# Convolution's layer norm: channel sums by a matrix of ones, and other banks for the memory's first values

## The chip, the cores and the metric

The kernel runs on one core of a Trainium2 chip. The metric is the device time of one execution in microseconds (us), the median over several runs.

## What is computed

Three blocks are applied to an activation of 512 tokens by 1024 channels, held transposed (channels on partitions, eight tiles of 128 by 512). The first block has a mixer, an attention over 256 memory rows, and a gated feed-forward net; the second has four feed-forward nets, a pooling mixer and a latent attention. The change lies in the mixer of the first block. The part that matters, cut:

```python
def parallel_mixer(h, w_in, conv_dw, conv_dw_b, conv_ln_g, conv_ln_b, q_norm_g, k_norm_g, w_out, tabs):
    z = jnp.einsum("bsd,dc->bsc", h, w_in)
    ...
    a = a_val * jax.nn.sigmoid(a_gate)
    a = dwconv_centred(a, conv_dw, conv_dw_b)     # 512 channels, 31 taps
    a = layernorm(a, conv_ln_g, conv_ln_b)        # over the 512 channels of a token
    a = jax.nn.silu(a)
    ...
    att = gqa_blocked(q, k, v)
    mixed = jnp.concatenate([a, att], axis=-1)
    return jnp.einsum("bsc,cd->bsd", mixed, w_out)

def layernorm(x, g, b):
    mu = jnp.mean(xf, axis=-1, keepdims=True)
    var = jnp.mean(jnp.square(xf - mu), axis=-1, keepdims=True)
    y = (xf - mu) * lax.rsqrt(var + EPS)
    return (y * g + b)
```

The memory attention that follows needs `kv = mem_n @ w_mem_kv`; its second half, the values, is made in two halves of 512 columns, the first of them inside the stretch that the change touches.

## The kernel before

**Arithmetic.** Each product with weights is made in three passes, high by high, high by low and low by high (`mm3`, L380 to L382), on fp32r tiles. Weights come as units of at most 128 by 1024. SyncE fetches a unit (`raw`), ScalarE makes its high part (`wh`, `high`, L364), VectorE its low part (`wl`, `low`, L372), and TensorE uses it. There are three buffers for each of `raw`, `wh` and `wl`: the high part of unit i waits until unit i-3 has been used, the fetch of unit i until the low part of unit i-3 is made. Units of w_mem_kv's value half 0 are v0 to v3 here; w_out's first units follow them, and are called w_out0 and w_out1 here.

**Order.** Nothing is scheduled dynamically. Each engine runs one list, in the order in which the functions `..._tensor`, `..._scalar`, `..._vector` and `..._gpsimd` are called in `program`, with semaphore waits between engines (`sig.at`, `sig.up`). A `Ring` hands out buffers or PSUM banks in turn, and a `take` names what must have freed the slot. The eight banks are main (0 to 2), score (3, 4), turn (5, 6) and out (7).

**Stages around the change.** `attend_*` runs the mixer's attention. Its last steps (t = 33 to 37) transpose the exponents of the last head (`value_turn_tensor`, L992), split them on ScalarE (L1001) and VectorE (L1006), and multiply them by the values (`value_tensor`). Beside that VectorE makes one tap of the convolution in each step (`tap_vector`, L626, the sums in bank 7), the last one being the last tap of channel tile 1; channel tiles 2 and 3 get their last taps on ScalarE and GpSimd (L638, L645). `value_vector` (L1057) divides the last output tile and so frees its main bank.

Then comes `layernorm_*`. `cv` holds the convolution's output, four tiles of 128 channels by 512 tokens. TensorE works on `mem_value_tensor(0, kk)`, one unit of the memory's values at a time, and between them on the layer norm: sums of `cv` with the data as the stationary operand and one column of ones moving (L1177), which gives token sums on partitions; VectorE adds and scales them (L1209, L1212); `spread_rows` (L474) transposes them back to a row for all partitions; VectorE subtracts (L1217, "centred"); ScalarE squares (L433); GpSimd adds two of the squares to the first (`add_square`, L438); `square_sums` (L449, L450) sums over channels; `mean_square` (L457) and `inverse_root` (L464, `ALU.pow` with exponent -0.5) work on 128 by 4 numbers; `spread_rows` again; VectorE multiplies (L1227), ScalarE does the Silu and the high part (L1200, L1202), VectorE the low part (L1231).

`post_product_tensor` then multiplies the eight mixed tiles by w_out. Its first step, `linear_pair`, goes over the eight tiles with w_out0 and w_out1 side by side, so from its first tile on it needs the low parts of both units; tiles 0 to 3 are the attention's, tiles 4 to 7 the convolution's.

Of the kernel before, what the change touches and what calls it, by code (L numbers as in the profile page):

```python
# [9 lines left out]
ALU = mybir.AluOpType  # L10
# [195 lines left out]
def f(ap):  # L206
    return ap.bitcast(F32)


def build(nc, wts, xT, memT, pos, cols, ident_d, perm_d, rope_d, pool_d, mask_d, out):  # L210
    with ExitStack() as ctx:
# [853 lines left out]
        def value_gpsimd(e, j):  # L1065
            e.wait_ge(*sig.at(("atth", j)))
            e.tensor_tensor(hxl[:, j, :], att_turn.of(("att", j))[:, :], f(hxh[:, j, :]), ALU.subtract) \
                .then_inc(*sig.up("att_low", ("mixed", j), ("free", ("att", j))))

        def attend_tensor(e):  # L1070
            for t in range(TURNS + 6):
                now, before = value_turn(t), value_turn(t - 1)
                if now:
                    value_turn_tensor(e, *now)
                if t < TURNS:
                    mix_score_tensor(e, t)
                if now and now[1] == 3 and now[0] % 2 == 1:
                    divisor_rows_tensor(e, now[0] // 2)
                if before:
                    value_tensor(e, *before)  # L1080
                if t < 5:
                    mem_key_tensor(e, 3 + t)

        def attend_scalar(e):
            k = 9
# [51 lines left out]
        def mem_value_tensor(e, half, kk):  # L1137
            i = U_VAL[half][kk]
            h, lo = weights_of(i)
            if kk == 0:  # L1140
                for tt in range(2):
                    _, old = mainb.take(("mv", half, tt))
                    e.wait_ge(*sig.at(old))
            e.wait_ge(*sig.at(("low", i)))
            for tt in range(2):
                b = mainb.of(("mv", half, tt))
                for k in range(2):
                    sh, sl, ready = mem_src(2 * kk + k)
                    e.wait_ge(*sig.at(ready))
                    made = mm3(e, b[:, :], (sh[:, tt * P:(tt + 1) * P], sl[:, tt * P:(tt + 1) * P]), (h[:, k, :], lo[:, k, :]),  # L1150
                               kk == 0 and k == 0, kk == 3 and k == 1)
            made.then_inc(*sig.up("unit_done", ("unit", i)))

        def mem_value_scalar(e, half):
            r = slice(half * 512, half * 512 + 512)
            e.wait_ge(*sig.at(("unit", U_VAL[half][3])))
            e.wait_ge(*sig.at(("score", TURNS - 1)))
            for tt in range(2):
                e.activation(mv_h[:, tt, r], mainb.of(("mv", half, tt))[:, :], ACT.Copy).then_inc(*sig.up("mem_value_high", ("mvh", half, tt)))

        def mem_value_vector(e, half):
            r = slice(half * 512, half * 512 + 512)
            for tt in range(2):
                e.wait_ge(*sig.at(("mvh", half, tt)))
                e.tensor_tensor(mv_l[:, tt, r], mainb.of(("mv", half, tt))[:, :], f(mv_h[:, tt, r]), ALU.subtract) \
                    .then_inc(*sig.up("mem_value_low", ("mv", half, tt), ("free", ("mv", half, tt))))

        CONV_LAST = [("tap", c, CONV_K - 1) for c in range(4)]

        def layernorm_tensor(e):  # L1170
            mem_value_tensor(e, 0, 0)
            o, old = turnb.take("conv mean")
            e.wait_ge(*sig.at(old))
            for c in range(4):
                e.wait_ge(*sig.at(CONV_LAST[c]))
                for i in range(4):
                    made = e.matmul(o[:, 4 * i + c:4 * i + c + 1], cv[:, c, i * P:(i + 1) * P], ones[:, 0:1], start=True, stop=True)  # L1177
            made.then_inc(*sig.up("conv_sums", "conv sums"))
            mem_value_tensor(e, 0, 1)
            spread_rows(e, "conv mean", "conv mean")  # L1180
            mem_value_tensor(e, 0, 2)
            square_sums(e, "conv", 3)
            spread_rows(e, "conv", ("root", "conv"))
            mem_value_tensor(e, 0, 3)

        def layernorm_scalar(e):
            for kk in range(2):
                high(e, U_VAL[0][kk] + 2)
            for c in range(4):
                square(e, "conv", c, cv[:, c, :], ("centred", c))  # L1190
            high(e, U_VAL[0][2] + 2)
            high(e, U_VAL[0][3] + 2)
            mem_value_scalar(e, 0)
            e.wait_ge(*sig.at(("free", ("pm", 6))))
            e.wait_ge(*sig.at(("free", ("pm", 7))))
            for c in range(4):
                s, old = silu_turn.take(("silu", c))
                e.wait_ge(*sig.at(old))
                e.wait_ge(*sig.at(("lnorm", c)))
                e.activation(s[:, :], cv[:, c, :], ACT.Silu, scale=col("conv_ln_g", c), bias=col("conv_ln_b", c)).then_inc(*sig.up("conv_silu", ("silu", c)))  # L1200
                e.wait_ge(*sig.at(("silu", c)))
                e.activation(hxh[:, 4 + c, :], s[:, :], ACT.Copy).then_inc(*sig.up("conv_high", ("convh", c)))  # L1202

        def layernorm_vector(e):
            low(e, U_VAL[0][0] + 2)
            st, old = stats.take(("st", "conv mean"))
            e.wait_ge(*sig.at(old))
            e.wait_ge(*sig.at("conv sums"))
            e.tensor_reduce(st[:, 0:4], turnb.of("conv mean")[:, 0:16].rearrange("p (i c) -> p i c", i=4), AX.X, ALU.add) \  # L1209
                .then_inc(*sig.up("conv_mean", "conv summed", ("free", "conv mean")))  # L1210
            e.wait_ge(*sig.at("conv summed"))
            e.tensor_scalar(st[:, 48:52], st[:, 0:4], 1.0 / S, None, ALU.mult).then_inc(*sig.up("conv_mean", "conv mean"))  # L1212
            low(e, U_VAL[0][1] + 2)
            for c in range(4):
                e.wait_ge(*sig.at(("rows", "conv mean")))
                e.wait_ge(*sig.at(CONV_LAST[c]))
                e.tensor_tensor(cv[:, c, :], cv[:, c, :], turnb.of(("rows", "conv mean"))[:, :], ALU.subtract) \  # L1217
                    .then_inc(*sig.up("centred", ("centred", c), *([("free", ("rows", "conv mean"))] if c == 3 else [])))
            low(e, U_VAL[0][2] + 2)
            mean_square(e, "conv", 1.0 / S)  # L1220
            low(e, U_VAL[0][3] + 2)
            mem_value_vector(e, 0)
            for c in range(4):
                e.wait_ge(*sig.at(("rows", "conv")))
                e.wait_ge(*sig.at(("sq", "conv", 3)))
                e.wait_ge(*sig.at(("centred", c)))
                e.tensor_tensor(cv[:, c, :], cv[:, c, :], turnb.of(("rows", "conv"))[:, :], ALU.mult) \  # L1227
                    .then_inc(*sig.up("conv_normed", ("lnorm", c), *([("free", ("rows", "conv"))] if c == 3 else [])))
            for c in range(4):
                e.wait_ge(*sig.at(("convh", c)))  # L1230
                e.tensor_tensor(hxl[:, 4 + c, :], silu_turn.of(("silu", c))[:, :], f(hxh[:, 4 + c, :]), ALU.subtract) \  # L1231
                    .then_inc(*sig.up("conv_low", ("mixed", 4 + c), ("free", ("silu", c))))

        def layernorm_gpsimd(e):
            for k in (1, 2):
                add_square(e, "conv", k)
            inverse_root(e, "conv")

# [1515 lines left out]
```

## Time and profile before

| | us |
|---|---|
| median of 3 runs (lowest, highest) | 2621.32 (2616.62, 2622.31) |
| profiled execution, whole time | 2623.71 |
| profiled execution, span from the first to the last instruction | 2622.4 |
| TensorE busy | 2566.9 |
| VectorE busy | 1225.3 |
| ScalarE busy | 934.4 |
| GpSimd busy | 620.9 |

Times in the profile are from the start of the span. Ends of matmuls are modelled and overlap the next matmul's start, so the distance between two starts is the better measure of what a matmul costs in a row of them. The stretch of the change goes from about 212 us to 262 us. In the profile PE is TensorE, DVE VectorE, ACT ScalarE, POOL GpSimd, PEclk the granted TensorE clock as a share of full speed.

### The profile page before, as it was taken

Reading aid. Unit: us, or ns where it says so; the run is one execution under the profiler, and the core shown is the slowest. Engines: PE = TensorE matmul, PEld = TensorE weight load, DVE = VectorE, ACT = ScalarE, POOL = GpSimd, SP = SyncE. Lnnn points to the kernel's source line nnn. Section 1 sums busy time; section 2 is a strip of 40 time slices with the busy share of each in tenths; the row PEclk is TensorE's granted clock in tenths of the full one; section 3 lists DMA queues with packets and bytes.
Section 4 is the critical chain, followed back from the end, with each engine's and each line's share of the span. In section 5 each row is a group of like instructions: output and inputs, shape, how many; then the busy total and the mean of one; then the engine's idle time right before and its main releaser. Section 6 shows DMA issues by size and latency. Waiting matters only on the chain.

```text
span 2622.4 us, 28823 instructions
## 1 busy us (share of the span) xinstructions
PE 2566.9 (98%) x11706; PEld 2097.2 (80%) x11706; DVE 1225.3 (47%) x1613; ACT 934.4 (36%) x1372; POOL 620.9 (24%) x471
## 2 busy tenths in 40 slices
PE   9898999999999999999999999999999999999999
PEld 7766777788887888888888888888788787888887
DVE  6896665555525333335333333333336565533322
ACT  4485343444423333224333222333223454333321
POOL 3663302222203222101222101222001431222200
PEclk9999999999999999999999999999999999999999
DMA  4211312333232233232333232333332111333232
GB/s 167 67 46 41 104 49 65 97 97 97 91 97 78 89 97 96 91 95 77 105 96 97 90 94 89 97 97 94 97 102 66 47 43 39 98 97 96 95 97 90
DMA packets 66484, 227.28 MB, mean 87 GB/s; under 512 B 7216, under 2 KB 8752, under 8 KB 66352
## 3 DMA queue, kind: packets, MB, share of 16 engines
q1 hardware_dynamic: 66352, 225.44, 27.4%
q8 instruction: 93, 1.52, 0.2%
q14 instruction: 39, 0.32, 0.0%
HBM read 223.31 MB, written 2.10 MB: 86 GB/s over the span
## 4 chain that ended last, share of the span: by engine, by line
PE 89%; DVE 6%; ACT 2%; issue 2%; POOL 0%; DMA 0%; SPq 0%; DVEq 0%; ACTq 0%; POOLq 0%
PE main L380 20%; PE main L381 19%; PE main L382 19%; PE score L380 7%; PE score L381 6%; PE score L382 6%; PE out L380 3%; PE out L381 3%; PE out L382 3%; DVE wl L372 1%; DVE cv L626 1%; PE main L1997 1%; PE turn L450 1%; PE turn L449 1%; DVE tmp L1313 1%
## 5 line engine op out<-in xcount | busy, mean ns | idle before, releaser
L372 DVE TENSOR_TENSOR wl<-raw,wh 128x1024 fp32r<-128x1024 f32 (+1 forms) x431 | 561.5, 1305 | 816.9 <-ACT wh L364 816.4
L364 ACT ACTIVATE wh<-raw 128x1024 fp32r<-128x1024 f32 (+1 forms) x431 | 440.3, 1025 | 612.4 <-PE main L382 503.5
L380 PE MATMUL main<-hxh,wh 128*128 128x512 f32 x1208 | 476.1, 394 | 8.6 <-DVE wl L372 3.3
L382 PE MATMUL main<-hxh,wl 128*128 128x512 f32 x1208 | 472.7, 391 | 0.0
L381 PE MATMUL main<-hxl,wh 128*128 128x512 f32 x1208 | 472.5, 391 | 0.0
L380 PE MATMUL main<-hh,wh 128*128 128x512 f32 x880 | 347.8, 395 | 1.5 <-DVE tmp L1604 0.8
L382 PE MATMUL main<-hh,wl 128*128 128x512 f32 x880 | 347.5, 395 | 0.0
L381 PE MATMUL main<-hl,wh 128*128 128x512 f32 x880 | 347.5, 395 | 0.0
L380 PEld LDWEIGHTS main<-hxh,wh 128*128 128x128 f32 x1208 | 228.1, 189 | 62.3 <-issue 8.1
L438 POOL TENSOR_TENSOR acc<-acc,sq 128x512 f32<-128x512 f32 (+1 forms) x84 | 120.1, 1430 | 648.8 <-ACT sq L433 643.9
L380 PE MATMUL score<-hxh,wh 128*128 128x512 f32 x664 | 261.2, 393 | 6.5 <-DVE wl L372 4.8
L382 PEld LDWEIGHTS main<-hxh,wl 128*128 128x128 f32 x1208 | 228.2, 189 | 48.2
L381 PEld LDWEIGHTS main<-hxl,wh 128*128 128x128 f32 x1208 | 228.3, 189 | 46.3
L1654 POOL TENSOR_TENSOR tmp<-tmp,tmp 128x512 f32<-128x512 f32 x88 | 113.6, 1291 | 627.4 <-DVE tmp L1604 590.3
L381 PE MATMUL score<-hxl,wh 128*128 128x512 f32 x664 | 259.2, 390 | 0.0
L382 PE MATMUL score<-hxh,wl 128*128 128x512 f32 x664 | 259.0, 390 | 0.0
L380 PEld LDWEIGHTS main<-hh,wh 128*128 128x128 f32 x880 | 165.3, 188 | 42.5 <-DVE tmp L1604 1.2
L382 PEld LDWEIGHTS main<-hh,wl 128*128 128x128 f32 x880 | 165.3, 188 | 39.9
L381 PEld LDWEIGHTS main<-hl,wh 128*128 128x128 f32 x880 | 165.3, 188 | 39.7
L1592 ACT ACTIVATE hh<-tmp 128x512 fp32r<-128x512 f32 x88 | 55.6, 632 | 324.9 <-POOL tmp L1654 324.9
L380 PEld LDWEIGHTS score<-hxh,wh 128*128 128x128 f32 x664 | 125.0, 188 | 36.8 <-DVE wl L372 4.1
L382 PEld LDWEIGHTS score<-hxh,wl 128*128 128x128 f32 x664 | 125.1, 188 | 26.4
(403 smaller groups left out, 3457.5 us busy)
## 6 DMA issues: line engine op xcount, KB each, us to landing
raw<-in_wts SPq DMA_DIRECT2D x375, 512.0 KB, 3.5
raw<-in_wts SPq DMA_DIRECT2D x52, 384.0 KB, 3.1
x<-in_xT SPq DMA_DIRECT2D x4, 512.0 KB, 7.2
out<-x SPq DMA_DIRECT2D x8, 256.0 KB, 3.9
memx<-in_memT SPq DMA_DIRECT2D x1, 1024.0 KB, 9.3
raw<-in_wts SPq DMA_DIRECT2D x4, 256.0 KB, 2.6
band<-in_pool SPq DMA_DIRECT2D x1, 768.0 KB, 4.5
rope<-in_rope SPq DMA_DIRECT2D x1, 512.0 KB, 6.8
```

Source lines behind the costliest of these rows:

```text
L364: e.activation(wh[i % NCONV][:, 0:n], raw[i % NRAW][:, 0:n], ACT.Copy).then_inc(*sig.up("weight_high", ("high", i)))
L372: e.tensor_tensor(wl[i % NCONV][:, 0:n], raw[i % NRAW][:, 0:n], f(wh[i % NCONV][:, 0:n]), ALU.subtract) \
L380: e.matmul(o, ah, bh, start=start, stop=False)
L381: e.matmul(o, ah, bl, start=False, stop=False)
L382: return e.matmul(o, al, bh, start=False, stop=stop)
L438: e.tensor_tensor(acc[:, 0:n], acc[:, 0:n], sq_turn(nm).of(("sq", nm, k))[:, 0:n], ALU.add) \
L449: e.matmul(o[:, i:i + 1], acc[:, r], ones[:, 0:1], start=True, stop=False)
L450: made = e.matmul(o[:, i:i + 1], s[:, r], ones[:, 0:1], start=False, stop=True)
L626: made = e.scalar_tensor_tensor(new_sum, a, w, old_sum, ALU.mult, ALU.add)
L1313: e.scalar_tensor_tensor(s[:, :], y[:, m, :], col(gain, m), turnb.of(("rows", nm))[:, :], ALU.mult, ALU.mult) \
L1592: e.activation(hh[:, c, :], s[:, :], ACT.Copy).then_inc(*sig.up("h_high", ("hh", nm, c)))
L1654: e.tensor_tensor(s1[:, :], s1[:, :], s2[:, :], ALU.mult).then_inc(*sig.up("h_joined", ("joined", nm, c), ("free", (nm, "us", c))))
```

## The change

- The sums of `cv` over channels are made with a 128 by 128 matrix of ones as the stationary operand and the whole tile (512 columns) moving, four matmuls that accumulate in a score bank. The result is the row of sums, the same on all partitions. The order is tiles 2, 0, 3, 1; three of the four stand in the last steps of the attention (t = 34, 35, 36), the last at the start of `layernorm_tensor`.
- Centring takes the sums from that bank with the factor -1/512 in one instruction per tile. The reduction, the scaling and the first `spread_rows` go.
- The squares are summed over channels in the same way, four matmuls, one for each tile of squares; GpSimd's two additions go.
- Mean square and inverse root are made on the whole row: VectorE writes 128 by 512 numbers to `rs`, GpSimd raises them to the power -0.5 there, and the second `spread_rows` goes.
- The first half of the memory's values gets banks 4 and 7 in place of two main banks.
- TensorE does v0, the sums of squares, then v1, v2, v3. ScalarE and VectorE copy the values out after the Silu and its low parts, not before. The low part of w_out1 is made between the first and second multiplication by `rs`.

```diff
+        def conv_mean_tensor(e, c):
+            if c == 2:
+                _, old = scoreb.take("conv mean")
+                e.wait_ge(*sig.at(old))
+            e.wait_ge(*sig.at(("tap", c, CONV_K - 1)))
+            made = e.matmul(scoreb.of("conv mean")[:, :], ones[:, 0:1].broadcast_to([P, P]), cv[:, c, :], start=c == 2, stop=c == 1)
+            if c == 1:
+                made.then_inc(*sig.up("conv_sums", "conv mean"))
+        value_banks = [Ring(banks[4:5] + banks[7:8]), mainb]
...
+                for c in {TURNS + 2: (2,), TURNS + 3: (0,), TURNS + 4: (3,)}.get(t, ()):
+                    conv_mean_tensor(e, c)
...
-                    _, old = mainb.take(("mv", half, tt))
+                    _, old = value_banks[half].take(("mv", half, tt))
...
         def layernorm_tensor(e):
+            conv_mean_tensor(e, 1)
             mem_value_tensor(e, 0, 0)
-            o, old = turnb.take("conv mean")
+            o, old = turnb.take(("sums", "conv"))
             e.wait_ge(*sig.at(old))
             for c in range(4):
-                e.wait_ge(*sig.at(CONV_LAST[c]))
-                for i in range(4):
-                    made = e.matmul(o[:, 4 * i + c:4 * i + c + 1], cv[:, c, i * P:(i + 1) * P], ones[:, 0:1], start=True, stop=True)
-            made.then_inc(*sig.up("conv_sums", "conv sums"))
-            mem_value_tensor(e, 0, 1)
-            spread_rows(e, "conv mean", "conv mean")
-            mem_value_tensor(e, 0, 2)
-            square_sums(e, "conv", 3)
-            spread_rows(e, "conv", ("root", "conv"))
-            mem_value_tensor(e, 0, 3)
+                e.wait_ge(*sig.at(("sq", "conv", c)))
+                s = sqs.of(("sq", "conv", c)) if c else acc
+                made = e.matmul(o[:, :], ones[:, 0:1].broadcast_to([P, P]), s[:, :], start=c == 0, stop=c == 3)
+            made.then_inc(...)
+            for kk in range(1, 4):
+                mem_value_tensor(e, 0, kk)

         def layernorm_scalar(e):
-            for kk in range(2):
-                high(e, U_VAL[0][kk] + 2)
+            high(e, U_VAL[0][0] + 2)
             for c in range(4):
                 square(e, "conv", c, cv[:, c, :], ("centred", c))
+            high(e, U_VAL[0][1] + 2)
             high(e, U_VAL[0][2] + 2)
             high(e, U_VAL[0][3] + 2)
-            mem_value_scalar(e, 0)
...
+            mem_value_scalar(e, 0)

         def layernorm_vector(e):
+            for c in range(4):
+                e.wait_ge(*sig.at("conv mean"))
+                e.scalar_tensor_tensor(cv[:, c, :], scoreb.of("conv mean")[:, :], -1.0 / S, cv[:, c, :], ALU.mult, ALU.add) \
+                    .then_inc(...)
             low(e, U_VAL[0][0] + 2)
...
+            t, old = rs_turn.take(("rs", "conv"))
+            e.wait_ge(*sig.at(old))
+            e.wait_ge(*sig.at(("sums", "conv")))
+            e.tensor_scalar(t[:, :], turnb.of(("sums", "conv"))[:, :], 1.0 / S, EPS, ALU.mult, ALU.add) \
+                .then_inc(...)
             low(e, U_VAL[0][1] + 2)
+            low(e, U_VAL[0][2] + 2)
             for c in range(4):
-                e.wait_ge(*sig.at(("rows", "conv")))
+                e.wait_ge(*sig.at(("root", "conv")))
                 e.wait_ge(*sig.at(("sq", "conv", 3)))
-                e.tensor_tensor(cv[:, c, :], cv[:, c, :], turnb.of(("rows", "conv"))[:, :], ALU.mult)
+                e.tensor_tensor(cv[:, c, :], cv[:, c, :], rs[:, :], ALU.mult)
+                if c == 0:
+                    low(e, U_VAL[0][3] + 2)
...
+            mem_value_vector(e, 0)

         def layernorm_gpsimd(e):
-            for k in (1, 2):
-                add_square(e, "conv", k)
-            inverse_root(e, "conv")
+            e.wait_ge(*sig.at(("ms", "conv")))
+            e.wait_ge(*sig.at("half"))
+            e.tensor_tensor(rs[:, :], rs[:, :], mhalf[:, 0:1].broadcast_to([P, S]), ALU.pow).then_inc(*sig.up("inverse_root", ("root", "conv")))
```

## Rows read from the trace of the kernel before

**Rows 1.** The page: busy time of each engine, and the chain by engine.

```profile
PE 2566.9 (98%) x11706; PEld 2097.2 (80%) x11706; DVE 1225.3 (47%) x1613; ACT 934.4 (36%) x1372; POOL 620.9 (24%) x471
...
PE 89%; DVE 6%; ACT 2%; issue 2%; POOL 0%; DMA 0%; SPq 0%; DVEq 0%; ACTq 0%; POOLq 0%
```

**Rows 2.** Busy time by stretch: length, engines' busy us, PEclk, DMA share, GB/s.

```profile
228.00:236.00 8.00, 5.98 (x29) 4.60 (x27) 4.59 (x7) 4.32 (x6) 2.55 (x2) 0.98 0.22 67
236.00:242.00 6.00, 3.58 (x18) 3.52 (x18) 2.00 (x3) 0.00 (x0) 1.93 (x1) 0.50 0.38 98
242.00:246.00 4.00, 4.00 (x13) 3.23 (x12) 0.00 (x0) 0.00 (x0) 0.00 (x0) 0.50 0.31 115
```

**Rows 3.** TensorE in order of time: start, us, engine, line, operation [idle before <-releaser].

```profile
215.42 0.60 PE L992 MATMUL turn<-ident,pm 128*128 128x128 f32 x4
...
218.92 0.50 PE L380 MATMUL main<-pt,vh 128*128 128x512 f32 x1 [0.27 <-DVE pt L1006]
...
221.02 0.47 PE L380 MATMUL main<-wh,mnh 128*128 128x512 f32 x1 [1.13 <-issue]
...
223.89 3.63 PE L1177 MATMUL turn<-ones,cv 128*128 128x1 f32 x32
227.38 0.48 PE L380 MATMUL main<-wh,mnh 128*128 128x512 f32 x1
...
235.68 0.56 PE L449 MATMUL turn<-ones,acc 128*128 128x1 f32 x2 [2.02 <-POOL acc L438]
...
241.65 1.08 PE L474 MATMUL turn<-ident,stat 128*128 128x128 f32 x4 [2.42 <-POOL stat L464]
...
245.94 0.42 PE L382 MATMUL main<-wh,mnl 128*128 128x512 f32 x1
...
248.52 0.48 PE L380 MATMUL main<-hxh,wh 128*128 128x512 f32 x1 [1.46 <-issue]
```

**Rows 4.** VectorE in order of time, the same stretch.

```profile
219.57 0.75 DVE L626 SCALAR_TENSOR_TENSOR cv<-apad,colsb,out 128x512 f32<-128x512 f32 x1
220.23 0.68 DVE L1057 TENSOR_TENSOR tmp<-main,tmp 128x512 f32<-128x512 f32 x1
...
230.90 2.48 DVE L1217 TENSOR_TENSOR cv<-cv,turn 128x512 f32<-128x512 f32 x4 [1.77 <-PE turn L474]
...
239.41 1.22 DVE L372 TENSOR_TENSOR wl<-raw,wh 128x1024 fp32r<-128x1024 f32 x1
```

**Rows 5.** ScalarE in order of time, the same stretch.

```profile
221.49 1.04 ACT L364 ACTIVATE wh<-raw 128x1024 fp32r<-128x1024 f32 x1
...
232.22 1.83 ACT L433 ACTIVATE sq<-cv 128x512 f32<-128x512 f32 x3
```

**Rows 6.** TensorE in order of time at 85 us, where an f32 matmul of 512 columns runs.

```profile
84.97 1.02 PE L744 MATMUL main<-tmp,perm 128*128 128x512 f32 x2
85.83 0.60 PE L738 MATMUL main<-ident,tmp 128*128 128x128 f32 x4
```

**Rows 7.** GpSimd in order of time: five powers on two, four and eight columns.

```profile
65.88 1.63 POOL L464 TENSOR_TENSOR stat<-stat,mhalf 128x2 f32<-128x2 f32 x1 [3.34 <-DVE stat L457]
72.89 1.64 POOL L825 TENSOR_TENSOR stat<-stat,mhalf 128x8 f32<-128x8 f32 x1 [5.39 <-DVE stat L797]
...
89.33 1.65 POOL L825 TENSOR_TENSOR stat<-stat,mhalf 128x8 f32<-128x8 f32 x1
...
239.57 1.93 POOL L464 TENSOR_TENSOR stat<-stat,mhalf 128x4 f32<-128x4 f32 x1 [3.95 <-DVE stat L457]
...
330.75 1.02 POOL L464 TENSOR_TENSOR stat<-stat,mhalf 128x4 f32<-128x4 f32 x1 [2.37 <-DVE stat L457]
```

**Rows 8.** VectorE in order of time, beside two of those powers.

```profile
65.72 1.21 DVE L372 TENSOR_TENSOR wl<-raw,wh 128x1024 fp32r<-128x1024 f32 x1
...
89.59 0.42 DVE L678 TENSOR_TENSOR mnl<-tmp,mnh 128x256 fp32r<-128x256 f32 x1 [0.48 <-ACT mnh L683]
```

**Rows 9.** The page's groups of instructions: GpSimd's additions and products of 512 columns.

```profile
L1654 POOL TENSOR_TENSOR tmp<-tmp,tmp 128x512 f32<-128x512 f32 x88 | 113.6, 1291 | 627.4 <-DVE tmp L1604 590.3
```

More of the change, by code:

```diff
@@ L1145, in mem_value_tensor @@
             for tt in range(2):
-                b = mainb.of(("mv", half, tt))
+                b = value_banks[half].of(("mv", half, tt))
                 for k in range(2):
@@ L1158, in mem_value_scalar @@
             for tt in range(2):
-                e.activation(mv_h[:, tt, r], mainb.of(("mv", half, tt))[:, :], ACT.Copy).then_inc(*sig.up("mem_value_high", ("mvh", half, tt)))
+                e.activation(mv_h[:, tt, r], value_banks[half].of(("mv", half, tt))[:, :], ACT.Copy).then_inc(*sig.up("mem_value_high", ("mvh", half, tt)))
         def mem_value_vector(e, half):
@@ L1164, in mem_value_vector @@
                 e.wait_ge(*sig.at(("mvh", half, tt)))
-                e.tensor_tensor(mv_l[:, tt, r], mainb.of(("mv", half, tt))[:, :], f(mv_h[:, tt, r]), ALU.subtract) \
+                e.tensor_tensor(mv_l[:, tt, r], value_banks[half].of(("mv", half, tt))[:, :], f(mv_h[:, tt, r]), ALU.subtract) \
                     .then_inc(*sig.up("mem_value_low", ("mv", half, tt), ("free", ("mv", half, tt))))
-        CONV_LAST = [("tap", c, CONV_K - 1) for c in range(4)]
         def layernorm_tensor(e):
+            conv_mean_tensor(e, 1)
             mem_value_tensor(e, 0, 0)
-            o, old = turnb.take("conv mean")
+            o, old = turnb.take(("sums", "conv"))
             e.wait_ge(*sig.at(old))
             for c in range(4):
-                e.wait_ge(*sig.at(CONV_LAST[c]))
-                for i in range(4):
-                    made = e.matmul(o[:, 4 * i + c:4 * i + c + 1], cv[:, c, i * P:(i + 1) * P], ones[:, 0:1], start=True, stop=True)
-            made.then_inc(*sig.up("conv_sums", "conv sums"))
-            mem_value_tensor(e, 0, 1)
-            spread_rows(e, "conv mean", "conv mean")
-            mem_value_tensor(e, 0, 2)
-            square_sums(e, "conv", 3)
-            spread_rows(e, "conv", ("root", "conv"))
-            mem_value_tensor(e, 0, 3)
+                e.wait_ge(*sig.at(("sq", "conv", c)))
+                s = sqs.of(("sq", "conv", c)) if c else acc
+                made = e.matmul(o[:, :], ones[:, 0:1].broadcast_to([P, P]), s[:, :], start=c == 0, stop=c == 3)
+            made.then_inc(*sig.up("sums_done", ("sums", "conv"), ("free", ("acc", "conv")), *(("free", ("sq", "conv", c)) for c in range(1, 4))))
+            for kk in range(1, 4):
+                mem_value_tensor(e, 0, kk)
         def layernorm_scalar(e):
-            for kk in range(2):
-                high(e, U_VAL[0][kk] + 2)
+            high(e, U_VAL[0][0] + 2)
             for c in range(4):
                 square(e, "conv", c, cv[:, c, :], ("centred", c))
+            high(e, U_VAL[0][1] + 2)
             high(e, U_VAL[0][2] + 2)
             high(e, U_VAL[0][3] + 2)
-            mem_value_scalar(e, 0)
             e.wait_ge(*sig.at(("free", ("pm", 6))))
@@ L1202, in layernorm_scalar @@
                 e.activation(hxh[:, 4 + c, :], s[:, :], ACT.Copy).then_inc(*sig.up("conv_high", ("convh", c)))
+            mem_value_scalar(e, 0)
         def layernorm_vector(e):
+            for c in range(4):
+                e.wait_ge(*sig.at("conv mean"))
+                e.scalar_tensor_tensor(cv[:, c, :], scoreb.of("conv mean")[:, :], -1.0 / S, cv[:, c, :], ALU.mult, ALU.add) \
+                    .then_inc(*sig.up("centred", ("centred", c), *([("free", "conv mean")] if c == 3 else [])))
@@ L1205, in layernorm_vector @@
             low(e, U_VAL[0][0] + 2)
-            st, old = stats.take(("st", "conv mean"))
+            t, old = rs_turn.take(("rs", "conv"))
             e.wait_ge(*sig.at(old))
[L1208 to L1212, printed above, removed]
+            e.wait_ge(*sig.at(("sums", "conv")))
@@ L1213, in layernorm_vector @@
+            e.tensor_scalar(t[:, :], turnb.of(("sums", "conv"))[:, :], 1.0 / S, EPS, ALU.mult, ALU.add) \
+                .then_inc(*sig.up("mean_square", ("ms", "conv"), ("free", ("sums", "conv"))))
             low(e, U_VAL[0][1] + 2)
+            low(e, U_VAL[0][2] + 2)
             for c in range(4):
[L1215 to L1223, printed above, removed]
-                e.wait_ge(*sig.at(("rows", "conv")))
+                e.wait_ge(*sig.at(("root", "conv")))
                 e.wait_ge(*sig.at(("sq", "conv", 3)))
-                e.wait_ge(*sig.at(("centred", c)))
-                e.tensor_tensor(cv[:, c, :], cv[:, c, :], turnb.of(("rows", "conv"))[:, :], ALU.mult) \
-                    .then_inc(*sig.up("conv_normed", ("lnorm", c), *([("free", ("rows", "conv"))] if c == 3 else [])))
+                e.tensor_tensor(cv[:, c, :], cv[:, c, :], rs[:, :], ALU.mult) \
+                    .then_inc(*sig.up("conv_normed", ("lnorm", c), *([("free", ("rs", "conv"))] if c == 3 else [])))
```

## Prediction

> **What bounds the kernel now.** I began with the page. TensorE is busy 98% of the span and carries 89% of the chain that ended last [rows 1]: TensorE sets the time, and an edit is worth what it does to TensorE's gaps and clock, or to the work that it must wait for. Then I read busy time by stretch over the stage that the diff touches. Most of the kernel is dense, but here are holes: from 236 to 242 us TensorE is busy 3.58 of 6 us at a granted clock of 0.50, and from 242 to 246 us it is busy throughout, still at 0.50 [rows 2], the lower of its two levels (1.2 GHz, not 2.4). TensorE's timeline says what it waited for: 1.13 us ahead of the first value product, 2.02 us for GpSimd's addition of squares, 2.42 us for GpSimd's power, 1.46 us ahead of the product with w_out, which starts at 248.52 [rows 3]. That start is the one number to follow: from there on the kernel's order stays as it is (up to the copies of the memory's values, which move behind the Silu), so a shift of this start is a shift of the end.
>
> **The sums over channels.** An f32 matmul of 512 columns takes two passes in this trace and holds TensorE for 85.83 - 84.97 = 0.86 us [rows 6]. The four of `conv_mean_tensor` cost 3.44 us, the sixteen they replace 227.38 - 223.89 = 3.49 [rows 3]: no gain in work, one in place. Three of them go into steps where TensorE now has little slack (0.27 us idle at 218.92), because transposition, ScalarE's copy, VectorE's subtraction and the value product follow one another. Two of the three stand ahead of a transposition that this chain needs (the one at 215.42 and the next [rows 3]), so they push it by up to 1.72 us; with 0.1 to 0.2 us of slack at a step I take 1.5. The last tap, which VectorE makes behind the subtraction, ends at 219.57 + 0.75 = 220.3 now [rows 4], and at 221.8 then. The fourth sum waits for it and runs from 221.9 to 222.8.
>
> **The banks.** The first value product waits at 221.02 for main banks that VectorE's L1057 (220.23 + 0.68) frees [rows 3, 4]. With banks 4 and 7 that wait goes, but the fourth sum now stands in front and waits for the last tap, which VectorE makes just before L1057. The edit gives nothing by itself. v0 then runs from 222.8 to 225.7 (a unit takes 223.89 - 221.02 = 2.87 us [rows 3]).
>
> **Centring and squares.** Centring needs the sums at 222.95 and takes four times 0.62 us (2.48 for four [rows 4]). ScalarE has the late copy of the attention and then one weight copy of 1.04 us first [rows 5], to 224.1, then four squares at 0.61 (1.83 for three [rows 5]), to 226.6. TensorE comes out of v0 at 225.7 with two squares done, so the four sums run in a row, 225.7 to 229.1. The two additions of GpSimd (to 235.68), the small power (until 241.65) and both transpositions of rows are gone from TensorE's path [rows 3]. v1, v2 and v3 follow without a gap, to 229.1 + 3 x 2.87 = 237.7. Their weights come in time: the low part of v2 directly after centring, of v3 after the mean square.
>
> If nothing else counted, the product with w_out could start at 237.7 rather than 248.5: 10.8 us gained. Part of that is clock, since TensorE would keep 2.4 GHz where 236 to 246 us was at half [rows 2]. The mean square now covers 512 columns and comes at 229.3 to 230.0 (0.68 us, as a pass over a bank in L1057 [rows 4]).
>
> **The power.** GpSimd now raises 512 columns, not four. The trace has it on 2, 4 and 8. Undisturbed, 4 columns take 1.02 us (330.75) and 8 take 1.64 and 1.65 [rows 7]; the slope is 0.63 / 4 = 0.157 us a column, the fixed part 0.39. The others look longer, and rows 8 say why. At 239.57 VectorE has just begun a low part of two SBUF inputs that ends at 239.41 + 1.22 = 240.63 [rows 4], and the power ends at 241.50, 0.87 behind it. At 65.88 the same instruction ends at 66.93 and the power on 2 columns ends at 67.51, 0.58 behind it [rows 7, 8]. The difference of 2 columns is 0.29 us, 0.145 a column: a second pair, with the port wait taken out, gives the same price. A power already running isn't held: VectorE's 0.42 us at 89.59 [rows 8] lies inside the one at 89.33, which takes 1.65 like its neighbour. So I read 2, 4 and 8 columns as one line, and carry it on: 0.39 + 512 x 0.157 = 80.8 us. Here too VectorE starts a low part (v3's) right after the mean square, which adds 1.93 - 1.02 = 0.9. The power runs from 230.0 to 311.7.
>
> Bounds: the nearest operation of this width on GpSimd, a product or a sum of 512 columns, takes 1.291 us [rows 9]; the whole 4-column time charged by column gives 512 x 1.02 / 4 = 130.6 us. I take 80.8 because the difference between sizes, not the size of one instruction, is the price of a column. A page holds a rule against this: the Trainium skill (GPSIMD Engine Reference, Elementwise — side-by-side cycle accounting) gives GpSimd about 2.6 cycles an element for a two-input operation, which would make this one some 1.1 us by estimate. By that rule the kernel gets faster (about 2610 us, rival 1 below), by the line slower (2689 us); the additions of rows 9 agree with the rule, the step from 4 to 8 columns of a power in rows 7 does not.
>
> **What waits behind it.** On VectorE the first multiplication by `rs`, and behind it in the same list the low part of w_out1. `linear_pair` needs w_out1 at its first tile, so TensorE can't even start on the attention's four tiles, which could have hidden 24 matmuls. The start is 311.7 + 0.62 + 1.22 [rows 4] + 0.2 for three hand-overs = 313.7. TensorE idles from 237.7 to 313.7, 76 us. The shift is 313.7 - 248.5 = 65.2 us. The convolution's tiles are ready (a multiplication, the Silu, two splits) while the pair works through the first four; copying the values out now falls before w_out2 is needed, 10.9 us into the pair. Both are hidden. After such a gap TensorE starts at 1.2 GHz. The row of before that shows such a restart goes from 241.65 to 245.94 [rows 3], 4.3 us at half speed, which loses 2.1 us; I add that.
>
> Sum: 65.2 + 2.1 = 67.3 us. The profiled execution took 2623.7 us (span 2622.4 and 1.3 around it), which gives 2691.0. The median of the runs is 2.4 us below that execution: 2688.6.
>
> **Rivals.** (1) *The power is cheap in bulk*: it works on columns as an addition does, once it has many. For: it has a fixed part, and nothing on chip shows it beyond 8 columns. Against: 2, 4 and 8 lie on one line. Its price is then 1.3 us [rows 9], and it ends at 230.0 + 0.9 + 1.3 = 232.2, before VectorE has even made the low part of w_out0, and the start is 237.7: 2621.3 - 10.8 = 2610.5, faster. It decides at a power of 311.7 - 65.2 - 230.0 = 16.5 us with its wait, or 0.03 us a column; 0.157 is five times that. (2) *Half the price*, as when columns overlap in a long run: 40 us less, 2648. For: two, four and eight are short runs. Against: no bend between them. (3) *The upper bound*, 130.6 us: 2738. Against: then 8 columns would have taken 2.04 us undisturbed.
>
> **How the numbers follow.** The line 0.80; cheap 0.09; half the price 0.07; the upper bound 0.03; a power near 16 us, that leaves the time within 0.2%, 0.01. A difference of 0.2%, 5 us, is about what a measurement of this kernel can tell from no change. Faster 0.09, same 0.01, slower 0.90. The predicted time is the line's, 2688.6. Its range: a column at 0.145, the other pair's price, takes 6 us off; a price that falls by a fifth over a long run takes 16 off and stands for part of rival 2; the restart at half clock may last twice as long (2 us), and if the power is held by VectorE more than once some 2 us come on top, with 6 more for what the stage after does with its weights late. That gives 2670 to 2699, which I widen to 2668 to 2700: it holds the 0.80 and leaves out the rest.
>
> **What the changed profile would show.** Right: one instruction on GpSimd of 128 by 512 of about 81 us, beginning near 230; TensorE empty from about 238 to 314, with w_out's product starting near 314 at a granted clock of 0.5; the chain of waits with GpSimd at 3% of the span where it was 0%; no TensorE gap longer than 1 us between 222 and 237. Wrong: that instruction below 16 us makes the kernel faster and the start lies near 238; if it is long and w_out's product starts earlier all the same, the low part of w_out1 isn't what I think it is. If v0 starts later than 223.5 the sums inside the attention cost more than 1.5 us.

## The result

The changed kernel takes 2689.1 us (median of 4 runs, 2687.1 to 2691.1) against 2620.9 us before (4 runs, 2616.6 to 2622.3): ratio 1.0266, 95% interval 1.0254 to 1.0278. It is 68 us slower. The forecast was 2688.6.

The page after, the lines that answer to [rows 1], and the new one of the chain by line:

```profile
PE 2560.5 (95%) x11666; PEld 2088.6 (78%) x11666; DVE 1226.5 (46%) x1611; ACT 933.1 (35%) x1372; POOL 697.4 (26%) x469
...
PE 87%; DVE 6%; POOL 3%; ACT 2%; issue 1%; DMA 0%; SPq 0%; DVEq 0%; ACTq 0%
PE main L380 19%; PE main L382 19%; PE main L381 19%; PE score L380 6%; PE score L382 6%; PE score L381 6%; POOL rs L1244 3%; PE out L380 3%; PE out L382 3%; PE out L381 3%; DVE wl L372 1%; DVE cv L626 1%; PE main L2004 1%; DVE tmp L1320 1%; PE turn L450 0%
```

TensorE's busy time hardly moves (6 us less); the span grows by 67.4. GpSimd enters the chain with 3%. The changed kernel's GpSimd in order of time shows what it is, and VectorE beside it (start, us, engine, line, operation, [idle before <-releaser]):

```profile
233.59 82.85 POOL L1244 TENSOR_TENSOR rs<-rs,mhalf 128x512 f32<-128x512 f32 x1 [5.64 <-DVE rs L1224]
```

```profile
224.56 0.75 DVE L626 SCALAR_TENSOR_TENSOR cv<-apad,colsb,out 128x512 f32<-128x512 f32 x1
...
232.82 0.69 DVE L1224 TENSOR_SCALAR rs<-turn 128x512 f32<-128x512 f32 x1 [2.68 <-PE turn L1192]
233.43 1.22 DVE L372 TENSOR_TENSOR wl<-raw,wh 128x1024 fp32r<-128x1024 f32 x1
...
316.48 0.69 DVE L1231 TENSOR_TENSOR cv<-cv,rs 128x512 f32<-128x512 f32 x1 [78.57 <-POOL rs L1244]
317.09 1.22 DVE L372 TENSOR_TENSOR wl<-raw,wh 128x1024 fp32r<-128x1024 f32 x1
```

And TensorE, to be read beside [rows 3]:

```profile
215.43 0.50 PE L380 MATMUL main<-pt,vh 128*128 128x512 f32 x1 [0.64 <-DVE pt L1006]
...
225.36 1.12 PE L1076 MATMUL score<-cv,ones 128*128 128x512 f32 x2 [0.18 <-DVE cv L626]
225.92 0.79 PE L380 MATMUL score<-wh,mnh 128*128 128x512 f32 x1
...
229.12 1.02 PE L1192 MATMUL turn<-acc,ones 128*128 128x512 f32 x2
229.97 2.74 PE L1192 MATMUL turn<-sq,ones 128*128 128x512 f32 x6
...
240.92 0.40 PE L380 MATMUL main<-hxh,wh 128*128 128x512 f32 x1
...
318.36 0.80 PE L380 MATMUL main<-hxh,wh 128*128 128x512 f32 x1 [76.57 <-DVE wl L372]
...
322.35 0.40 PE L380 MATMUL main<-hxh,wh 128*128 128x512 f32 x1
```

The reader is to see three things. From the fourth sum of the mean to the last value product there is no gap where the kernel before had three (1.13, 2.02 and 2.42 us [rows 3]). At 240.92 TensorE starts on w_out, does the three passes of w_out0's first tile, and then stands for 76.57 us; the releaser named is VectorE's low part, not the power, since w_out1's low part is what the next pass needs. And after the gap the passes are 0.43 us apart until 322.35, 0.23 after it. The stretches (length, busy us of TensorE, weight loads, VectorE, ScalarE, GpSimd, PEclk, DMA share, GB/s):

```profile
238.00:312.00 74.00, 3.79 (x17) 2.72 (x15) 0.00 (x0) 1.06 (x1) 74.00 (x1) 0.54 0.02 7
312.00:318.00 6.00, 0.00 (x0) 0.00 (x0) 1.52 (x2) 0.75 (x1) 4.45 (x1) 0.50 0.00 0
```

This execution reaches the stage 3.6 us later than that of before: the value product with 0.64 us of idle time stands at 215.43, its like before at 211.80. The change has touched nothing up to there, so comparisons inside the stage are made from that product on. The end of the stage is taken at GpSimd's next power on 4 columns, behind the product with w_out, here in the kernel before and in the changed one:

```profile
297.13 1.94 POOL L464 TENSOR_TENSOR stat<-stat,mhalf 128x4 f32<-128x4 f32 x1 [8.26 <-DVE stat L457]
```

```profile
368.15 1.94 POOL L464 TENSOR_TENSOR stat<-stat,mhalf 128x4 f32<-128x4 f32 x1 [8.25 <-DVE stat L457]
```

So counted, the stage takes 85.3 us before and 152.7 after.

### The profile page after: what moved, and what is told of

It is laid out like the page before. It is cut to its first block, busy times and chain, and to the rows that moved or that the text cites. A ratio compares the mean times of both kernels' runs of the same rounds, so it can differ in the third digit from the quotient of the medians.

```text
span 2689.8 us, 28731 instructions
## 1 busy us (share of the span) xinstructions
PE 2560.5 (95%) x11666; PEld 2088.6 (78%) x11666; DVE 1226.5 (46%) x1611; ACT 933.1 (35%) x1372; POOL 697.4 (26%) x469
## 4 chain that ended last, share of the span: by engine, by line
PE 87%; DVE 6%; POOL 3%; ACT 2%; issue 1%; DMA 0%; SPq 0%; DVEq 0%; ACTq 0%
PE main L380 19%; PE main L382 19%; PE main L381 19%; PE score L380 6%; PE score L382 6%; PE score L381 6%; POOL rs L1244 3%; PE out L380 3%; PE out L382 3%; PE out L381 3%; DVE wl L372 1%; DVE cv L626 1%; PE main L2004 1%; DVE tmp L1320 1%; PE turn L450 0%
## 5 line engine op out<-in xcount | busy, mean ns | idle before, releaser
L380 PEld LDWEIGHTS score<-hxh,wh 128*128 128x128 f32 x664 | 125.3, 189 | 36.7 <-DVE wl L372 5.1
```

What stands on the lines that cost most here:

```text
L380: e.matmul(o, ah, bh, start=start, stop=False)
```

## The experiments

Ratios are to the kernel before, run on the same chip in the same rounds: its median was 2621.5 us beside the first four kernels, 2621.8 beside the next four and 2619.7 beside the last four. Medians of different groups are compared by way of these.

| kernel | median us | runs | ratio, 95% interval |
|---|---|---|---|
| product for the power | 2610.1 | 5 | 0.9956, 0.9940 to 0.9972 |
| small root | 2612.2 | 8 | 0.9966, 0.9953 to 0.9978 |
| w_out1 first | 2686.1 | 4 | 1.0252, 1.0236 to 1.0268 |
| power on 256 columns | 2649.8 | 1 | |
| mean only | 2608.6 | 4 | 0.9949, 0.9932 to 0.9965 |
| banks only | 2622.3 | 1 | |
| width sweep | 2616.1 | 1 | |
| before, low part first | 2619.7 | 1 | |
| small root, ring advanced | 2609.3 | 5 | 0.9961, 0.9949 to 0.9974 |
| changed kernel, ring advanced | 2684.1 | 4 | 1.0246, 1.0232 to 1.0260 |
| banks only, ring advanced | 2621.0 | 10 | 0.9998, 0.9988 to 1.0009 |
| sums late | 2607.7 | 1 | |

**A product in place of the power.**

```diff
-            e.tensor_tensor(rs[:, :], rs[:, :], mhalf[:, 0:1].broadcast_to([P, S]), ALU.pow)
+            e.tensor_tensor(rs[:, :], rs[:, :], mhalf[:, 0:1].broadcast_to([P, S]), ALU.mult)
```

> The changed kernel, with the power on 512 columns replaced by a product on the same 512 columns (the inverse root is left out, so the convolution half is not normalised). Theory A, the price of the power alone makes the kernel slower: GpSimd's instruction takes about 1.3 us plus up to 0.9 of waiting for VectorE, TensorE goes from the last value product to w_out's product without a gap, and the time is 2610 to 2612 us, 0.4% under the kernel before. Theory B, the reordered stage has a wait of its own: the time stays at 2621 us or above, with a TensorE gap between the value products and w_out's product.

```profile
230.88 1.95 POOL L1244 TENSOR_TENSOR rs<-rs,mhalf 128x512 f32<-128x512 f32 x1 [5.62 <-DVE rs L1224]
```

2610.1 us. One operation code, same operands and same waits, is worth 79 us. The instruction falls from 82.85 to 1.95 us, and TensorE has no gap between the last sum of the mean and w_out's product. The stage takes 74.0 us, 78.7 less than in the changed kernel and 11.3 less than before. Theory B is out: the reordered stage has no long wait of its own.

**The small root.** The squares are summed to 16 columns, the power works on 128 by 4, `spread_rows` follows v1; everything else stays changed.

```diff
-                made = e.matmul(o[:, :], ones[:, 0:1].broadcast_to([P, P]), s[:, :], start=c == 0, stop=c == 3)
+                for i in range(4):
+                    made = e.matmul(o[:, 4 * i + c:4 * i + c + 1], s[:, i * P:(i + 1) * P], ones[:, 0:1], start=True, stop=True)
...
+            mem_value_tensor(e, 0, 1)
+            spread_rows(e, "conv", ("root", "conv"))
...
+            inverse_root(e, "conv")
```

> The changed kernel with only its root undone: the squares are summed to 16 single columns and the power works on 128 by 4, then one transposition to rows; sums of the mean by the matrix of ones, banks and order stay changed. Theory A: the power takes 1.0 to 1.9 us and hides under the second value product, 2610 to 2612 us. Theory B, the three sums inside the attention and the later copies eat what the order saves: 2619 to 2622 us.

```profile
230.04 1.92 POOL L464 TENSOR_TENSOR stat<-stat,mhalf 128x4 f32<-128x4 f32 x1 [5.34 <-DVE stat L1230]
```

2612.2 us, 0.34% faster than before, at the edge of what theory A gave. The power hides under v1. But v1 itself runs in part at half clock here, though TensorE doesn't stand (columns as above):

```profile
230.00:234.00 4.00, 4.00 (x14) 3.03 (x13) 1.09 (x1) 0.00 (x0) 1.92 (x1) 0.57 0.41 129
```

With the product in place of the power, and the sums of squares over the whole row, the granted clock is 1.00 from 227 to 238 us. There w_out's product starts 25.5 us behind the value product, here 27.6. The kernel before makes its sums of the mean in single columns too and keeps 1.00 behind them (228 to 231 us), so why the clock falls here stays open.

**w_out1 first.**

```diff
             low(e, U_VAL[0][2] + 2)
+            low(e, U_VAL[0][3] + 2)
             for c in range(4):
...
-                if c == 0:
-                    low(e, U_VAL[0][3] + 2)
```

> The changed kernel with the low part of w_out1 ahead of the first multiplication by the inverse root. Theory A, the product with w_out waits for w_out1 and not for its data: the attention's four tiles (24 matmuls) run before the power ends, the wait moves to the convolution's first tile, about 4 us are gained, 2685 us. Theory B, the wait was for data all along: 2689 us, no change.

```profile
317.92 0.80 PE L380 MATMUL main<-hxh,wh 128*128 128x512 f32 x1 [74.29 <-DVE hxl L1236]
```

2686.1 us, 3.0 us less than the changed kernel where about 4 were expected; the intervals of the two ratios (1.0236 to 1.0268 and 1.0254 to 1.0278) overlap, so the times alone would not show it. The stage does: 150.3 us against 152.7. The wait now names `hxl`, the convolution's first tile, and is shorter because the four tiles of the attention run ahead of it. The order of VectorE's list was a small part of the damage, 2.5 us; the power is the rest.

**The power on 256 columns.**

```diff
-            e.tensor_tensor(rs[:, :], rs[:, :], mhalf[:, 0:1].broadcast_to([P, S]), ALU.pow)
+            e.tensor_tensor(rs[:, 0:256], rs[:, 0:256], mhalf[:, 0:1].broadcast_to([P, 256]), ALU.pow)
```

> The changed kernel with the power on 256 of the 512 columns (the other 256 columns keep the mean square, so they are not normalised). Theory A, a constant price by column of 0.157 us: GpSimd's instruction takes about 0.39 + 40.2 + 0.9 = 41.5 us and the kernel 2649 us. Theory B, a price by instruction or one that bends with width: the instruction is clearly not half of 82.85 us.

```profile
230.85 42.05 POOL L1244 TENSOR_TENSOR rs<-rs,mhalf 128x256 f32<-128x256 f32 x1 [5.62 <-DVE rs L1224]
```

42.05 us against 82.85: 256 columns more cost 40.8 us, 0.159 each. The kernel takes 2649.8 us.

**The width sweep.**

```diff
             inverse_root(e, "mem")
+            for n, wd in enumerate((8, 16, 32, 64, 128)):
+                e.wait_ge(*sig.at(("sweep", n)))
+                e.tensor_tensor(swept[:, 0:wd], swept[:, 0:wd], mhalf[:, 0:1].broadcast_to([P, wd]), ALU.pow).then_inc(*sig.up("sweep", ("sweep", n + 1)))
```

> The kernel before with five more powers on GpSimd in the memory attention, where it is idle, on 8, 16, 32, 64 and 128 columns of a tile of its own (they feed nothing). Theory A, a constant price by column of 0.157 us and 0.39 fixed: 1.65, 2.9, 5.4, 10.4 and 20.5 us. Theory B, cheaper columns in longer runs: the step from 64 to 128 columns is clearly under 10 us. The kernel's time is not the point; some us more are possible.

The instructions of that line one by one (count, duration ns min/median/max, start, shape); the last row is the last two together, of which 20729 ns are the 128 columns':

```profile
L1473 POOL TENSOR_TENSOR qraw<-qraw,mhalf x1: 1635/1635/1635, 331.3 to 331.3; 128x8 f32<-128x8 f32 x1
L1473 POOL TENSOR_TENSOR qraw<-qraw,mhalf x1: 2896/2896/2896, 333.0 to 333.0; 128x16 f32<-128x16 f32 x1
L1473 POOL TENSOR_TENSOR qraw<-qraw,mhalf x1: 5415/5415/5415, 336.0 to 336.0; 128x32 f32<-128x32 f32 x1
L1473 POOL TENSOR_TENSOR qraw<-qraw,mhalf x1: 10521/10521/10521, 341.5 to 341.5; 128x64 f32<-128x64 f32 x1
L1473 POOL TENSOR_TENSOR qraw<-qraw,mhalf x2: 10521/15625/20729, 341.5 to 352.1; 128x64 f32<-128x64 f32 x1, 128x128 f32<-128x128 f32 x1
```

The steps are 1.26, 2.52, 5.11 and 10.21 us for 8, 16, 32 and 64 columns: 0.158, 0.157, 0.160 and 0.160 us each. There is no bend that makes columns cheaper in a long run; above 32 they cost about 1% more. The tile was filled with 2.0, and the price by column is the one that the changed kernel pays on its own numbers. Beside the last three powers VectorE made low parts of 1.23 us (the first of them at 340.36), and these powers kept to the line.

**Before, with the low part of w_out1 first.**

```diff
+            low(e, U_VAL[0][3] + 2)
             mean_square(e, "conv", 1.0 / S)
-            low(e, U_VAL[0][3] + 2)
```

> The kernel before with the low part of w_out1 ahead of the convolution's mean square instead of behind it. Theory A, GpSimd's power on 128 by 4 takes 1.93 us there because VectorE's instruction with two SBUF inputs holds its port at the start: the power takes 1.02 us and w_out's product starts about 0.9 us earlier. Theory B, the 1.93 us is GpSimd's own (code or data): it stays at 1.93.

```profile
238.72 1.02 POOL L464 TENSOR_TENSOR stat<-stat,mhalf 128x4 f32<-128x4 f32 x1 [3.93 <-DVE stat L457]
```

```profile
239.88 1.09 PE L474 MATMUL turn<-ident,stat 128*128 128x128 f32 x4 [1.51 <-POOL stat L464]
```

1.02 us in place of 1.93 [rows 7], and TensorE's wait for it 1.51 in place of 2.42 [rows 3]: the 0.9 us is VectorE's instruction with two SBUF inputs at the start of the power. Only 0.5 us of it arrive: w_out's product starts 36.2 us behind the value product, against 36.7 before.

**The mean only.** The kernel before with the four sums by the matrix of ones (three inside the attention) and centring from their bank; squares, additions on GpSimd, root and banks as before.

```diff
+                for c in {TURNS + 2: (2,), TURNS + 3: (0,), TURNS + 4: (3,)}.get(t, ()):
+                    conv_mean_tensor(e, c)
...
+            conv_mean_tensor(e, 1)
             mem_value_tensor(e, 0, 0)
-            o, old = turnb.take("conv mean")
...
-            spread_rows(e, "conv mean", "conv mean")
```

> The kernel before with the first part of the change alone: the four sums of the mean by the matrix of ones (three inside the attention), centring from their bank. Squares are still added on GpSimd, summed by columns, the power works on 128 by 4, and the values' copies stay ahead of the Silu. Theory A: the squares come about 5 us earlier, the root's sums follow v2 almost without a gap, w_out's product starts about 8 us earlier, 2613 us. Theory B, the sums inside the attention cost what the earlier centring gives: 2620 us or more. Theory C, most of the gain of the version with the small root comes from the sums of squares and not from the mean: 2617 to 2619 us.

```profile
235.96 0.75 PE L474 MATMUL turn<-ident,stat 128*128 128x128 f32 x4 [2.33 <-POOL stat L464]
...
242.42 0.47 PE L380 MATMUL main<-hxh,wh 128*128 128x512 f32 x1 [1.46 <-issue]
```

2608.6 us, 0.51% faster than before, and 4 us better than I expected of it. GpSimd's additions are hidden under v1 and v2, and w_out's product starts at 242.42 where it was 248.52, and counted from the value product (212.50 here) 6.8 us earlier, where about 8 were expected. The 2.9 us in the latent attention (below) are in the whole time too. It still waits 2.33 us for the root and 1.46 us ahead of w_out, which the small root's version does not, and yet it is not slower than that version. So something in the other edits had to cost time elsewhere.

**The banks only.**

```diff
-                    _, old = mainb.take(("mv", half, tt))
+                    _, old = value_banks[half].take(("mv", half, tt))
```

> The kernel before with only the banks of the memory's first values changed to 4 and 7. Theory A: the first value product starts when the last tap frees bank 7, 0.6 us ahead of where it starts now, and the convolution's chain behind it is not shorter by more; the single run is within 2617 to 2623 us. Theory B, the wait ahead of that product was for weights or for the instruction itself: it stays at 1.1 us.

```profile
221.06 0.50 PE L380 MATMUL score<-wh,mnh 128*128 128x512 f32 x1 [0.48 <-DVE cv L626]
...
254.86 0.50 PE L380 MATMUL main<-hxh,wh 128*128 128x512 f32 x1 [0.72 <-DVE hxl L1233]
```

The wait ahead of the first value product falls from 1.13 to 0.48 us, and the 1.46 us ahead of w_out's product, which I had put down to nothing, are gone too: it was a main bank that the values' copies free late. Inside w_out's product 0.72 us for the convolution's tile come back. All the same the stage isn't shorter. w_out's product starts 36.0 us behind the value product against 36.7, 0.7 us earlier, and the end of the stage comes 0.5 us later, 85.8 against 85.3. What the waits give is lost in the clock, which falls during v1, where before it was 1.00 (228 to 231 us):

```profile
227.00:231.00 4.00, 4.00 (x15) 3.28 (x15) 1.47 (x3) 0.00 (x0) 0.00 (x0) 0.57 0.26 65
```

The kernel at 2622.3 us isn't faster either. I compared the stages one by one, from one inverse root to the next. The first feed-forward net, from the root at its start to the root at its end (471.51 to 823.46 before), falls into two groups:

| kernel | us | first values in |
|---|---|---|
| before | 351.95 | main banks |
| mean only | 351.92 | main banks |
| width sweep | 351.87 | main banks |
| before, low part first | 350.75 | main banks |
| changed kernel | 357.91 | banks 4 and 7 |
| product for the power | 357.27 | banks 4 and 7 |
| small root | 356.31 | banks 4 and 7 |
| w_out1 first | 357.50 | banks 4 and 7 |
| power on 256 columns | 357.71 | banks 4 and 7 |
| banks only | 356.54 | banks 4 and 7 |

In the changed kernel one wait stands there, and the versions with the small root and with the banks only have the same 4.0 us:

```profile
770.35 0.80 PE L380 MATMUL main<-hh,wh 128*128 128x512 f32 x1 [4.04 <-DVE pad L1537]
```

It is the first matmul of the net's down product. The values no longer take two turns of the main ring, so every later user of that ring gets a bank two places on, and here it is the bank in which the net's last tile still waits for VectorE.

**The ring advanced.** The same edit on three kernels: the changed one, the small root's, the banks' alone.

```diff
                     _, old = value_banks[half].take(("mv", half, tt))
                     e.wait_ge(*sig.at(old))
+                if half == 0:
+                    mainb.n += 2
```

> The changed kernel with the main ring advanced by two turns, nothing else. Theory A: the same 4 to 5 us go, 2684 to 2685 us. Theory B: 2689 us.

> The version with the small root and the other banks, with the main ring advanced by the two turns that the values no longer take, so that all later stages get the main banks that they have in the kernel before. Theory A, the feed-forward net's down product waits 4.0 us for VectorE only because its first bank is the one of the last tile: that wait goes, 2607 to 2608 us, the fastest so far, and no TensorE gap of 4 us near the end of that net. Theory B, the wait has another cause (the stage starts at another time): it stays, 2612 us.

> The kernel before with banks 4 and 7 for the first values and the main ring advanced by two turns. Theory A, the banks alone are worth the wait ahead of w_out's product, less what then waits for the convolution's tiles: about 1 us, 2620 us, against 2622.3 for the banks without the advance; in the profile no 4 us gap. Theory B: no difference to the banks without the advance.

The 4 us wait is gone in all three. The net takes 353.1, 351.9 and 353.0 us. That is 4.8, 4.4 and 3.5 us less in this net. The whole times show less of it. The changed kernel falls from 2689.1 to 2684.1 us, as theory A said, but measured against the kernel before in its own rounds it is 64.4 us slower where it was 68.2: 3.8 us. The small root's is 10.3 us faster where it was 9.3, the banks' alone 1.3 us slower where a single run gave 0.5. The intervals of the two ratios overlap for the changed kernel (1.0254 to 1.0278, 1.0232 to 1.0260) and for the small root's. So the wait and its end are shown in the traces of the net, and a gain of the whole kernel isn't shown. The banks alone, ring advanced, leave the time where it was: 0.9998, 0.9988 to 1.0009. Their stage takes 87.4 us, 2.0 more than before, with the granted clock at 0.50 from 226 to 231 us, so of a gain by the banks alone nothing is seen.

**The sums late.** The small root's version, ring advanced, with all four sums of the mean behind the attention.

```diff
-                for c in {TURNS + 2: (2,), TURNS + 3: (0,), TURNS + 4: (3,)}.get(t, ()):
-                    conv_mean_tensor(e, c)
...
-            conv_mean_tensor(e, 1)
+            for c in (2, 0, 3, 1):
+                conv_mean_tensor(e, c)
```

> The version with the small root, other banks and advanced ring, with all four sums of the mean after the attention instead of three inside it. Theory A, the attention's chain gets its 1.4 us back but the four sums then stand in a row of 3.4 us behind the last value product: the first product of the memory's values starts 0.3 to 0.5 us later than with the sums inside, no difference in the time. Theory B, the sums inside the attention are a net loss: it starts earlier.

```profile
213.75 0.50 PE L380 MATMUL main<-pt,vh 128*128 128x512 f32 x1 [0.64 <-DVE pt L1006]
...
221.68 3.60 PE L1076 MATMUL score<-cv,ones 128*128 128x512 f32 x8
224.71 0.79 PE L380 MATMUL score<-wh,mnh 128*128 128x512 f32 x1
```

From the value product with 0.64 us of idle time to the first product of the memory's values it is 10.96 us here and 10.49 with the sums inside (215.43 to 225.92 in the changed kernel): 0.5 us later, as theory A had it. One run at 2607.7 us doesn't tell it from 2609.3.

## Why the prediction was right

**The price of the power** was the step on which all hung. 0.157 us a column from 2, 4 and 8 columns gave 80.8 us; with VectorE's 0.9 in front 81.7; measured 82.85. The sweep shows the line up to 128 columns and the changed kernel to 512; above 32 columns a column is 0.160, which is the 1.2 us that were missing. Rival 1 (cheap in bulk), rival 2 (half the price) and rival 3 (the upper bound) are refuted by the sweep. The product in the power's place took 1.95 us, beside a VectorE instruction, and such a product takes 1.29 on average [rows 9]; the power on the same operands took 82.85. The Trainium skill (GPSIMD Engine Reference, Elementwise — side-by-side cycle accounting) gives about 2.6 cycles an element for a two-input operation, some 1.1 us for 512 columns by estimate. The product's 1.29 us comes near it, the power's 82.85 does not. What rival 1 gave for the time, 2610.5 us, is what the product in its place took, 2610.1. Its stage is 11.3 us shorter than before (10.8 in the sum), and what the later stages add and take cancels there too.

**The stage, term by term**, counted from the value product at 211.80 and 215.43: the last tap ends at 221.7 on before's clock (221.8 expected), the power starts at 230.0 (230.0), w_out's product would start at 237.3 (237.7), the gap is 76.6 us (76). The shift of w_out's product is 102.9 - 36.7 = 66.2 us, less 0.7 for the three passes already done, 65.5 (65.2). The restart at half clock lasts 4.0 us and costs 1.8 (2.1). The row that the 2.1 came from was no clean restart, since the clock was at 0.50 from 236 us on, ahead of that gap [rows 2]; that it fitted is partly luck.

**Where it was only lucky.** The sum of the stage was right; that the whole came within 0.5 us was luck. The profiled span grew by 67.4 us: 3.6 before the stage is reached, 67.4 in it (85.3 to 152.7), and 3.6 less in all that follows. There the first feed-forward net takes 6.0 us more, the latent attention 2.9 less, the heads' stage behind it (2029.76 to 2267.63 before) 4.3 less and everything else together 2.4 less. I had put nothing down for any of these. The first follows from the change, and the second seems to: "from there on the kernel's order stays as it is" was true of the order and not of the banks.

- The banks "give nothing by itself" came true for the time and was wrong as an account. They take away the 1.46 us ahead of w_out's product, which stand with the mean only and not with the banks only; my sum had these without saying from where. In the feed-forward net they cost 4 us of waiting, 3.5 to 4.8 us of that net, which the sum had not. The three pairs with the ring advanced show it.
- The sums of the mean take one turn of the score ring. In the latent attention, 1.8 ms later, a key product then gets another score bank. Before, at the first such product, and after:

```profile
2023.17 0.39 PE L380 MATMUL score<-wh,ckh 128*128 128x256 f32 x1 [2.27 <-DVE tmp L1900]
```

```profile
2097.82 0.39 PE L380 MATMUL score<-wh,ckh 128*128 128x256 f32 x1 [0.86 <-DVE tmp L1907]
```

The releaser is the loop over the latent's banks, one bank earlier; the granted clock around it is 0.82 before (2020.0 to 2029.7 us) and 1.00 after, and the stage from 1991.57 to 2029.76 takes 38.19 us before and 35.3 in each of the kernels with the new sums, 36.7 to 38.2 in those without. That the turn of the ring is the cause is argued from these rows; no run here advanced the score ring alone.

The rest is spread: the heads' stage that follows takes between 232 and 238 us over the fourteen profiles without following any edit, and that is a good part of why small differences between these kernels (2607.7 to 2612.2) can't be ordered. The mean alone, with two waits more in its stage, takes 78.6 us for it, the small root with the ring advanced 76.1: part of what the missing waits save there goes in the clock during v1. The profiled spans, 2607.1 and 2605.1 us, show that difference, the medians don't.

**Which version is best.** The mean only (0.9949) and the small root with the ring advanced (0.9961) both beat the kernel before and the changed one; their intervals overlap, and overlap that of the small root without the advance (0.9966).

## What to carry to other kernels

Ask of each widened instruction what one column costs on its engine, by taking two sizes of it from the trace and their difference, and take waits for another engine's instruction out first: a power on 4 columns at 1 to 2 us looked like overhead, and 0.63 of its undisturbed 1.02 us was the price of the four columns. The transposition that keeps a slow elementwise function on 4 columns in place of 512 is cheap: it held TensorE for 0.36 us (233.76 to 234.12) in the version with the small root. And when buffers come from rings, moving one user off a ring moves every later user by as many places: compare all stages of the two profiles, not only the one that was edited, and the granted clock in each beside the waits.

## What the runs showed of the hardware

- GpSimd's power (`tensor_tensor` with `ALU.pow`) takes 0.158 us a column up to 32 columns and 0.160 beyond, 128 partitions at once, with 0.38 us fixed; a product on 512 columns takes 1.29 us undisturbed [rows 9].
- A power on GpSimd that starts beside a VectorE instruction with two SBUF inputs waits until that one ends, 0.9 us here (1.93 and 1.02 us for the same power); one that is already running isn't held (20.73 us for 128 columns beside VectorE's low parts, on the line of the others).
- After 76.6 us of idle time TensorE ran 4.0 us at 1.2 GHz, no longer than after the gap of 2.4 us in the kernel before, where the rest at half clock was 4.3 us [rows 3] and the clock had been at half from 236 us on [rows 2].
- The granted clock can fall with no TensorE gap in front: 0.57 during v1 (230 to 234 us) with the small root and 0.57 (227 to 231 us) with the banks only, both behind sums in single columns, and 1.00 at the same place in the kernel before.
